# A hybrid retention and sliding-window layer: keys, queries, probabilities and gates turned through DRAM and on DVE instead of on TensorE

## The reference

```python
h = rmsnorm(x, norm_g) * (1 + scale) + shift          # scale, shift, gate from the condition
rq, rk, rv, rg, aq, ak, av, ag = split(h @ w_in)      # 1024 x 3328
# retention, 4 heads of 128, in blocks: scores times a decay, plus a state carried from block to block
s = (rope(rq) @ rope(rk).T) * decay;  out = s @ rv + (rq @ R) * q_dec;  R = g**L * R + (k * k_dec).T @ rv
r = headnorm(out) * silu(rg)
# attention, 8 query heads of 64 over 2 key heads, a window of 128 + 64 keys, with a learned sink
m = max(max_k(s), sink);  p = exp(s - m);  a = (p / (sum(p) + exp(sink - m))) @ av * silu(ag)
x = x + gate * (concat(r, a) @ w_out);  y = rmsnorm(x, final_g)
```

## Time and profile before

| | us |
|---|---|
| median of 3 runs | 1991.48 |
| the profiled execution | 1995.48 |
| its span, first to last instruction | 1993.7 |
| TensorE busy | 1938.5 (97%) |
| DVE busy | 1089.7 (55%) |
| ACT busy | 634.3 (32%) |
| POOL busy | 150.9 (8%) |
| phase A, from the first dense product to the change of phase | about 70 to 918 |
| phase B | about 918 to 1994 |
| DMA | 222.22 MB, 111 GB/s, 460480 packets, of them 405016 under 512 B |
| mean granted clock | 0.989 |

### The profile page before, as it was taken

How to read it: one execution, slowest core, us unless ns; L and a number is a source line. 1 busy time by engine, 2 the same in 40 slices (tenths; PEclk the granted TensorE clock), 3 DMA queues, 4 the chain that set the end, 5 groups by cost and what they waited for, 6 DMA issues and landing times.

```text
span 1993.7 us, 30575 instructions
## 1 busy us (share of the span) xinstructions
PE 1938.5 (97%) x10240; PEld 1596.4 (80%) x10240; DVE 1089.7 (55%) x2507; ACT 634.3 (32%) x1537; POOL 150.9 (8%) x340
## 2 busy tenths in 40 slices
PE   4999999999999999998899999999999999999997
PEld 2778888888888888887688888888888888888885
DVE  3645555555555555566455555545555554555554
ACT  2312222222222221233334333333434334343332
POOL 0000000000000000000000000000000000000000
PEclk8999999999999999999899999999999999999999
DMA  9654444444444444436424243332424333242431
GB/s 350 206 142 118 117 111 115 108 110 120 120 120 120 110 111 116 108 99 184 127 69 116 63 110 82 92 105 68 116 68 105 88 86 106 67 116 70 104 79 35
DMA packets 460480, 222.22 MB, mean 111 GB/s; under 512 B 405016, under 2 KB 412376, under 8 KB 459424
## 3 DMA queue, kind: packets, MB, share of 16 engines
q1 hardware_dynamic: 460448, 221.81, 40.8%
HBM read 137.33 MB, written 84.42 MB: 111 GB/s over the span
## 4 chain that ended last, share of the span: by engine, by line
PE 91%; issue 3%; DMA 2%; DVE 2%; SPq 1%; ACT 0%; POOL 0%; POOLq 0%; DVEq 0%; ACTq 0%
PE bank L1140 74%; PE bank L1331 3%; PE bank L1314 3%; PE bank L1302 2%; PE bank L1303 2%; PE bank L1272 1%; PE bank L1213 1%; PE bank L1214 1%; PE bank L1218 1%; DMA fin_g<-in_final_g 1%; PE bank L1390 1%; PE bank L1261 1%; DMA xn_scratch<-xn 1%; SPq L386 0%; PE bank L1415 0%
## 5 line engine op out<-in xcount | busy, mean ns | idle before, releaser
L1140 PE MATMUL bank<-wh,hh 128*128 128x512 f32 x1584 | 407.3, 399 | 7.6 <-ACT wh L311 4.4
L1140 PE MATMUL bank<-wl,hh 128*128 128x512 f32 x1584 | 397.4, 393 | 0.0
L1140 PE MATMUL bank<-wh,hl 128*128 128x512 f32 x1584 | 397.2, 393 | 0.0
L1140 PEld LDWEIGHTS bank<-wl,hh 128*128 128x128 f32 x1584 | 294.9, 188 | 74.0 <-issue 12.3
L1140 PEld LDWEIGHTS bank<-wh,hl 128*128 128x128 f32 x1584 | 295.7, 188 | 62.0
L1140 PEld LDWEIGHTS bank<-wh,hh 128*128 128x128 f32 x1584 | 291.2, 190 | 65.9 <-ACT wh L311 4.7
L646 ACT ACTIVATE hf<-xn,tiny_a 128x128 f32<-128x128 f32 (+1 forms) x248 | 98.6, 480 | 383.3 <-DVE xn L817 383.3
L709 ACT ACTIVATE s_row<-s_row,tiny_b 128x256 f32<-128x256 f32 x264 | 131.1, 498 | 151.0 <-DVE tiny_b L1001 151.0
L1140 PE MATMUL bank<-wh,yh 128*128 128x512 f32 x528 | 149.7, 405 | 2.2 <-DVE yl L1085 2.2
L1140 PE MATMUL bank<-wh,yl 128*128 128x512 f32 x528 | 146.1, 399 | 0.0
L1140 PE MATMUL bank<-wl,yh 128*128 128x512 f32 x528 | 143.5, 394 | 0.0
(11 more groups left out here) (151 smaller groups left out, 2532.2 us busy)
## 6 DMA issues: line engine op xcount, KB each, us to landing
xt<-in_x_prompt SPq DMA_DIRECT2D x64, 512.0 KB, 3.9
h_scratch<-hf SPq DMA_DIRECT2D x33, 512.0 KB, 2.9
hf<-h_scratch SPq DMA_DIRECT2D x33, 512.0 KB, 4.5
out<-xt SPq DMA_DIRECT2D x32, 512.0 KB, 2.9
xn_scratch<-xn SPq DMA_DIRECT2D x31, 512.0 KB, 2.9
xp<-xn_scratch SPq DMA_DIRECT2D x124, 128.0 KB, 3.5
aq_scratch<-aq_row SPq DMA_DIRECT2D x31, 512.0 KB, 3.5
aq_row<-aq_scratch SPq DMA_DIRECT2D x124, 128.0 KB, 3.6
```

Source lines behind the costliest of these rows:

```text
L1140: ins = mm(out, a[:, k, :], b[:, k, :], start=first and n == part[0] and k == chunks[0], stop=last and n == part[-1] and k == chunks[-1])
```

## The change

Phase A: the keys no longer pass through TensorE's transposes (but for the first and the sample tile). SP stores `k_row` to `k_scratch` and loads it back by blocks into the first half of `xp`; DVE transposes it at the head of its next slot. The xp blocks of the next tile wait for that transpose. The scores leave the end of the slot and stand behind the next tile's first dense product, followed by the state update and the outputs, state product first.

Phase B: TensorE makes no transposes. The tile's attention is one slot longer in flight: slot t projects tile t, attends tile t-1 and does the output product of tile t-2, undivided. Queries and keys go out in one tensor (`aqk`, 160 columns by 4 blocks), probabilities in two halves (`p`), gates in one (`g`). `store_blocks` stores 32 partitions a DMA and places the blocks in DRAM, so that each load back is one DMA of whole rows; DVE transposes within the blocks. Queries are split into high and low parts after the turn, so scores take three products instead of two, each of 64 rows on one half of the array (`tile_position`). Banks, buffers and masks are laid out anew; POOL no longer shifts the keys.

The diff, cut to its core:

```diff
@@ SP, phase A slot
                 if not static(i) or 1 <= t < SAMPLE:
                     wait(sp, xn_stored, 16 * t)
+                    wait(sp, kt_done, t)
                     load_blocks(xp, xn_dram[t + 1], xp_loaded)
...
                     wait(sp, yr_done, t)
                     sp.dma_start(yr_dram[t - 1], r_out[:, :]).then_inc(yr_stored, 16)
+                if not pe_turns(i, t) and (not static(i) or t < SAMPLE):
+                    wait(sp, k_done, t + 1)
+                    sp.dma_start(k_dram[t], k_row[:, :]).then_inc(k_stored, 16)
+                    wait(sp, k_stored, 16 * t)
+                    wait(sp, x_turned, t)
+                    load_blocks(k_in, k_dram[t], k_loaded)
@@ SP, phase B
+            def store_blocks(dst, src, stored):
+                for i in range(4):
+                    sp.dma_start(dst.rearrange("(b r) (i n) -> r b i n", r=32, i=4)[:, :, i, :],
+                                 src[32 * i:32 * (i + 1)]).then_inc(stored, 16)
+            def slot_b(i, u):
...
                 if not static(i) or 1 <= t < SAMPLE:
                     wait(sp, b_split, t + 1)
                     sp.dma_start(hf[:, :, :].rearrange("p k r -> p (k r)"), h_dram[t + 1]).then_inc(hb_loaded, 16)
+                if not static(i) or t >= 3:
+                    wait(sp, fin_done, t - 2)
...
+                        sp.dma_start(y_prompt[bass.ts(t - 3, P), :], xts[1 - u][:, :]).then_inc(y_stored[1 - u], 16)
...
+                    wait(sp, yr_turned, t - 1)
+                    load_blocks(yr_in, yr_dram[t - 1], yr_loaded)
...
+                    for half in range(2):
+                        wait(sp, exp_done, 2 * (t - 1) + half + 1)
+                        store_blocks(p_dram[2 * (t - 1) + half], s_row[:, half], p_stored[half])
+                if mid:
+                    wait(sp, y_stored[1 - u], 16 * (i - 1 + u))
...
+                        sp.dma_start(xts[1 - u][:, :], x_prompt[bass.ts(t - 1, P), :]).then_inc(xb_loaded[1 - u], 16)
+                if mid:
+                    wait(sp, p_stored[0], 4 * 16 * t)
+                    sp.dma_start(p_in[:, 0].rearrange("p b n -> p (b n)"), p_dram[2 * (t - 1)]).then_inc(p_loaded[0], 16)
+                    wait(sp, gate_scaled, t)
+                    store_blocks(g_dram[t - 1], a_gates[1 - u][:, :].rearrange("p (b n) -> p b n", b=4), g_stored)
+                if front:
+                    wait(sp, kv_done, t + 1)
+                    wait(sp, aq_done, t + 1)
...
+                    store_blocks(aqk_dram[t], aqk_row, aqk_stored)
...
+                if mid:
+                    wait(sp, p_stored[1], 4 * 16 * t)
+                    sp.dma_start(p_in[:, 1].rearrange("p b n -> p (b n)"), p_dram[2 * (t - 1) + 1]).then_inc(p_loaded[1], 16)
+                    wait(sp, g_stored, 4 * 16 * t)
+                    sp.dma_start(a_gates[1 - u][:, :], g_dram[t - 1]).then_inc(g_loaded, 16)
+                if front:
+                    wait(sp, aqk_stored, 4 * 16 * (t + 1))
...
+                    sp.dma_start(aqk_row[:, :, :].rearrange("p b n -> p (b n)"), aqk_dram[t]).then_inc(aqk_loaded, 16)
@@ DVE, phase A slot
+                if not static(i) or 2 <= t <= SAMPLE:
+                    wait(dve, k_loaded, 4 * 16 * (t - 1))
+                    wait(dve, s_ready, t - 1)
+                    V.transpose(k_t[:, :], k_in).then_inc(kt_done, 1)
                 if more:
                     normalise(*nxt)
+                if back:
+                    wait(dve, s_ready, t)
+                    wait(dve, out_ready, t - 1)
+                    V.tensor_tensor(s_t[:, :], qs_b[:, :], decay[:, :], ALU.mult).then_inc(st_done, 1)
@@ TensorE, phase A slot, behind the first dense product
+                    wait(pe, st_done, t - 1)
+                    wait(pe, qt_done, t)
+                    wait(pe, kt_done, t)
                     for h in range(RH):
                         c = slice(h * DK, (h + 1) * DK)
+                        last = mm(qs_b[:, c], k_t[:, c], q_t[:, c], start=True, stop=True)
+                    last.then_inc(s_ready, 1)
+                    wait(pe, state_done, t - 1)
+                    wait(pe, v_done, t)
...
                         last = mm(upd_b[:, c], k_row[:, c], v_dec[:, c], start=True, stop=True)
                     last.then_inc(upd_ready, 1)
...
+                        mm(out_b[:, c], q_t[:, c], st[:, c], start=True, stop=False)
+                        wait(pe, st_done, t)
+                        last = mm(out_b[:, c], s_t[:, c], v_row[:, c], start=False, stop=True)
+                    last.then_inc(out_ready, 1)
@@ TensorE, phase B
+            def scores(i, u):
...
+                wait(pe, qk_hi, t + 1)
+                wait(pe, qk_lo, t + 1)
+                for half in range(2):
+                    wait(pe, s_masked, 2 * (t - 1) + half + 1)
+                    for jl in range(2):
+                        for n, (q, k) in enumerate(((aq_h, ak_h), (aq_h, ak_l), (aq_l, ak_h))):
+                            for g in range(2):
+                                rows = slice(g * HD, (g + 1) * HD)
+                                last = mm(s_banks[2 * half + g][:, jl * 2 * P:(jl + 1) * 2 * P], q[rows, 2 * half + jl, :],
+                                          k[rows, :, :], start=n == 0, stop=n == 2, tile_position=(g * HD, 0))
+                    last.then_inc(sb_ready, 1)
...
+            slot order: scores(t-1); dense keys/values(t); dense queries(t); dense gates(t);
+                        output product group 2, group 3 (t-2); weigh(t-1)
```

More of the change, by code:

```diff
@@ L986, in mask_max @@
                 n = 2 * t + half + 1
[L987 removed]
                 wait(dve, sb_ready, n)
+                wait(dve, pt_done, n - 2)
                 wait(dve, sarg_done, n - 1)
[L990 removed]
+                m = mask[:, 2 if static(i) and t == 0 else u, :]
                 V.memset(spare, 0.0)
@@ L1349, in retention_out_1 @@
-                def retention_out_1(part=(0, 1, 2)):
-                    wait(pe, aq_lo, t + 1 if front else t)
-                    ins = dense(zb1[:, :], yh, yl, group(3), part=part, chunks=range(4), first=part[0] == 0, last=False)
-                    if part[-1] == 2:
-                        ins.then_inc(yr_used, 1)
-                first = static(i) and t == 0
-                if front and not first:
-                    dense_kv(i, u)
-                if back:
-                    scores(*prev, 0)
-                    if not front:
-                        wait(pe, o0_read, t - 1)
-                        retention_out_0()
@@ L1418, in slot_b @@
-                if back:
-                    if front:
-                        retention_out_1(part=(2,))
-                    wait(pe, ya_lo, t)
-                    dense(zb0[:, :], yh, yl, group(2), chunks=range(4, 8), first=False).then_inc(o0_ready, 1)
-                    dense(zb1[:, :], yh, yl, group(3), chunks=range(4, 8), first=False).then_inc(o1_ready, 1)
-            phase_tiles(pe, slot_b, SAMPLE + 1)
+                if mid and not (static(i) and t == 1):
+                    scores(*prev)
```

694 lines of the change are left out of this document (311 added, 383 removed).

## The result

The changed kernel takes 2033.26 us (2032.95 to 2037.48, 4 runs) against 1991.65 (1989.26 to 1993.56, 4 runs) beside it: ratio 1.0213, 95% interval 1.0197 to 1.0229. It is slower, as forecast, but by 41.6 us and not by 108.5. Its profiled span is 2035.7 us, 42.0 over that of before. All ratios compare fast executions only; one of the ten executions of experiment 2's kernel, of 6512 us, is outside them.

What follows compares the result with a forecast made beforehand. Phase B is bound by a circle through SyncE's queue, DRAM and DVE, 34.6 us a tile: 1995.5 - 8 (phase A) + 92 (31 slots) + 6 (start) + 19 (end) = 2104.5, 2100 on the median's scale; range 1965 to 2155.

Steps and rivals of the forecast that it cites:

- step 2: Phase B, SyncE: p, gate and query/key stores with p0 load, 15 issues of 0.66 plus 0.45, 10.4 us.
- step 1: Phase B, SyncE after its wake (0.2): y store, yr blocks and x load, 4.4 us.
- step 3: Phase B: last store lands 3.4, reload 3.6, DVE's turning of p, gate and h split end 0.8 later; 7.8 us.
- step 4: Phase B: DVE turns queries and keys, ACT makes high parts, DVE the low ones; 2.4 us.
- step 5: Phase B, DVE: output gating and adds, four of 0.69 us with gaps; 3.0 us.
- step 6: Phase B, next slot on DVE: ya, two mask/max groups, ya_lo and final; 6.5 us.
- the circle holds but is short: Rival, phase B: at 0.4 to 0.5 us an issue a tile takes 31.3 to 32.6; 1998 to 2038 us; chance 0.14.
- The likeliest case: The forecast itself: phase B's circle at 0.66 us an issue, 34.6 us a tile, 2100 us; chance 0.52.
- TensorE's tile: Phase B: dense 24.9, weighing 2.0, scores 2.6 and 0.1 make 29.6 us (28.4 to 29.9), hidden under the circle.
- circle of 25.5: Phase A: xn, h, rope, yr and k trips through SyncE's queue, landings and DVE; 25.7 us a tile taken, 8 gained.
- DVE has p1 in hand before 25 us into the tile: Phase B: sign that the forecast is wrong, the probabilities' second half reaching DVE that early.
- Start and end: Phase B: first queries and keys also through DRAM, +6 us; last tile's longer final path after its scores, +19 us.

Runs made afterwards that it cites:

- experiment 2: Kernel before, with phase A's scores moved behind the next tile's first dense product and the keys' transposes kept on TensorE: 1990.85 us, ratio 0.9994.
- experiment 4: Changed kernel with four more 32-partition stores a tile on SyncE's queue behind the query/key stores: 2067.07 us, ratio 1.0374.
- experiment 5: Changed kernel with the y store, yr block loads and x load moved to the end of SyncE's slot: 1892.90 us, ratio 0.9505.
- experiment 6: Changed kernel with the eight stores of probabilities issued from ACT's queue instead of SyncE's: 1942.90 us, ratio 0.9752.
- experiment 8: Changed kernel with each half of the probabilities stored by one whole-row transfer instead of four (wrong row order): 1984.29 us, ratio 0.9968.
- experiment 14: Changed kernel with gates and queries/keys stored by one whole-row transfer each instead of four (wrong outputs): 2005.11 us, ratio 1.0069.
- experiment 12: Changed kernel with out store and x load in phase B's loop cut to 512 of 1024 columns (outputs not whole): 2027.97 us, ratio 1.0178.
- experiment 1: Kernel before with phase A's edit alone (keys through DRAM, scores moved): 1978.86 us, ratio 0.9932.

## Why the prediction was right in its sign and wrong in its size

- **What limits phase B** was right: the circle through SyncE's queue, DRAM and DVE, its six steps in their order, TensorE waiting at the first scores for DVE's low parts (90.0 us in 27 stops) and DVE for the p reload (10.95 and 2.56 us in the tile shown). The trace's chain of waits and experiments 4, 5, 6, 8 and 14, each of which moved the time in the direction the circle says, bear it out.
- **The step that failed is step 2, the price of an issue**: 15 issues of 0.66 plus 0.45 were to take 10.4. Eight stores of 32 partitions take 4.09 and four 1.92 and 1.90, about 0.5 each (0.51 for the eight) where the block load's four in 2.93 gave 0.73. I took 0.66 because both partial forms in the trace of before were loads or a cache row at 0.59 to 0.73; a store of 32 partitions is cheaper than both and lies in the middle of the range I kept. From the first store of p to the start of the last query/key store is 9.0 us, 8.6 without the x load that step 1 holds: -1.8, or -55 us over 31 slots, which came out 56.6 below the forecast's +92. That the two agree so well is in part luck: step 3 gave 0.6 back, and the mean tile is 0.45 shorter than the one read here.
- The other steps of the same tile, measured against forecast: step 1 4.3 (4.4); step 3, from 1409.40 to DVE's turning of queries and keys at 1417.81, 8.4 (7.8); step 4 2.6 (2.4); step 5 2.9 (3.0); step 6 6.4 (6.5). Sum 33.4 with the wake of 0.2 (34.6); the mean slot, 32.90, is 1.7 under the forecast's. Step 3 was too short since the last half of p landed in 5.1 us (4.5 on the mean) and not in the 3.9 read from an x load.
- **What I had not seen**: I held the issues to be the whole of the queue's part, one more us on the queue being one on the tile. Experiments 4, 8 and 14 give 1.0 of 1.9, 1.6 of 3.3 and 0.9 of 3.1 us; in experiment 8 a wait of 1.2 for a store's landing is most of what is missing. The landing is not a constant beside the queue. That the DMA engines' own load explains this fits the windows of three runs. Half the bytes of y and x changed little (experiment 12), so I take it to be the work of the small pieces in the stores and reloads of p, gates and queries rather than bytes as such. No run changed the size of pieces alone, so this last step is not shown.
- **The rival "the circle holds but is short"** (0.4 to 0.5 an issue, 1998 to 2038, chance 0.14) is what happened in its price, 0.51 and so at its upper end. That its time holds the 2033 too is luck: the 31 slots came out at +35.4, above its +30, and the rest at +6.6 instead of +17. The likeliest case and this one differ by the price only.
- **TensorE's tile** was put at 29.6 (28.4 to 29.9). It hid under the circle in the changed kernel; experiment 5 shows 28.35. The scores' pairs run side by side, 1.6 and not 2.6 us; the lower bound of 1.4 was the right end. The rule that the Trainium skill states (TensorEngine Tiling (Array Packing), Key Properties), tiles in parallel and a drain at a change of mode, agrees in its first half: 0.12 us a pair. The 24 scores take 0.2 us more than 12 pairs, which is no more than compatible with the drain.
- **Phase A**: -8 forecast, -22.0 measured. The saving of 0.5 a tile was right (25.97 to 25.47 in experiment 1, 25.37 in the changed kernel); the step that failed is the 25.7 that I took for a circle of 25.5 and for the wait for the decay, and neither shows: TensorE is 797.12 of 800 us busy. Another 4 to 6 us come from `small`, an edit of one number that stands in the diff and in no term of the sum.
- **The signs of being wrong.** "DVE has p1 in hand before 25 us into the tile" came true, at 18.6 us (1414.94 less 1396.37). But the forecast's own sum puts it near 19 (0.2, 4.4, 10.4 and a landing of 3.9), so this sign was set wrongly and says nothing. A partial store cost neither 0.6 or more nor 0.4 or less. TensorE waited 90.0 us at the scores and 20.6 us, in 14 stops, for DVE's turned p at weighing.
- **Start and end**: +4.2 and +24.4 against +6 and +19, the same mechanism. At the end TensorE stands twice for DVE's yl. Eight products then last 3.78 us instead of 1.98, at a granted clock of 0.50 (1989.88 to 1993.50):
```profile
1989.88 3.78 PE L1171 MATMUL bank<-wh,yh 128*128 128x512 f32 x8 [9.23 <-DVE yl L1052]
...
2013.94 3.78 PE L1171 MATMUL bank<-wh,yh 128*128 128x512 f32 x8 [6.28 <-DVE yl L1052]
```

## What to carry to other kernels

Where data makes a round trip through DRAM inside a tile, write down the circle and ask for each transfer on its queue whether anybody in the circle waits for it; those for which nobody does go behind the last that somebody waits for. Six issues moved in this way took a kernel 2% slower than its original to 5% faster, while making issues fewer (experiments 8 and 14) paid only a quarter to a half of their queue time: a store's landing showed in one, and the DMA engines were nearly full in the same stretch in both. And look at every number of a diff: a tile 64 bytes wider was worth 4 to 8 us of 2000.

## What the runs showed of the hardware that was not expected

- A store of 32 partitions holds SyncE's queue 0.53 us from start to start (eight last 4.09 us), a block load of 32 partitions 0.77 (four last 2.93). A whole-row transfer lasts 0.33 to 0.45, with 0.1 to 0.3 to the next.
- The landing of the same 512 KB reload took 3.8 us on the mean with four issues more ahead of it, 4.5 in the changed kernel and 6.7 with six fewer, there also in whole rows. In the tiles shown the share of the DMA engines during it was 0.69, 0.95 and 0.95, so the share alone doesn't give the landing.
- Moving eight stores to ACT's queue gave 2.8 of the 4.1 us that they held SyncE. The Trainium skill (DMA: Bandwidth & Descriptors, Issuing engines are not separate DMA queues) says that this saves only the time to start the DMAs, "usually small relative to the DMA itself". The first half agrees; here that time, summed over the tiles, was worth 90 us of 2033.
- Eight dense products of 512 columns take 1.81, 1.83 or 1.87 us by where in SBUF one operand's buffer starts (moved by 64, 0 and 32 bytes a partition); the shifts of 32 and 64 bytes moved the end of phase A by +3.3 and -6.2 us.
